# Expert 0's column selection and row gather placed ahead of the last tile's norm, and one ScalarE scaling placed later

## What is computed

```python
x = layer_norm(DN_ALPHA * x + merged @ w_out[l], ln1_g[l], ln1_b[l])
moe = grouped_moe(x, w_router, b_router, w_gate, w_up, w_down)
x = layer_norm(DN_ALPHA * x + moe, ln2_g[l], ln2_b[l])

# grouped_moe
gates = shared_group_router(xt, w_router, b_router)     # two of 16 are not zero for a token
for e in range(N_EXPERTS):
    h = jax.nn.silu(xt @ w_gate[e]) * (xt @ w_up[e])     # 1024 -> 512
    out = out + gates[:, e:e + 1] * (h @ w_down[e])      # 512 -> 1024
```

## Time and profile before

| | |
|---|---|
| median of 3 runs | 828.04 us (827.35 to 828.05) |
| profiled execution | 828.57 us, its span 826.9 us |
| TensorE busy | 814.5 us (99%) |
| VectorE busy | 574.3 us (69%) |
| ScalarE busy | 454.9 us (55%) |
| GpSimd busy | 82.7 us (10%) |
| memory read, written | 163.49 MB, 16.30 MB |

### The profile page before, as it was taken

One profiled execution on the slowest core, in us unless ns is written; L12 is line 12 of the kernel. 1 busy time (PEld: TensorE's weight loads), 2 busy tenths in 40 slices (PEclk: granted clock), 3 DMA queues, 4 the chain that ended last, 5 costly groups with the idle time before them and its releaser, 6 DMA issues.

```text
span 826.9 us, 11020 instructions
## 1 busy us (share of the span) xinstructions
PE 814.5 (99%) x3809; PEld 677.9 (82%) x3809; DVE 574.3 (69%) x672; ACT 454.9 (55%) x462; POOL 82.7 (10%) x78
## 2 busy tenths in 40 slices
PE   9999999999999999999999999999999999999995
PEld 8888888888888888888888888888888888888873
DVE  5877445434557885431455688899899898999857
ACT  5655524434466663333233333588787888878742
POOL 1000000100000000000000000633111011000037
PEclk9999999999999999999999999999999999999998
DMA  7332334553233323334432926599999999999592
GB/s 228 89 103 84 102 91 146 197 178 101 76 102 101 101 82 114 88 101 132 154 95 76 352 107 255 173 329 413 410 371 405 399 398 381 402 390 395 224 349 102
DMA packets 112358, 173.51 MB, mean 210 GB/s; under 512 B 7418, under 2 KB 90019, under 8 KB 100550
## 3 DMA queue, kind: packets, MB, share of 16 engines
q1 hardware_dynamic: 106502, 159.80, 54.4%
q0 software_dynamic: 5824, 13.30, 4.4%
HBM read 163.49 MB, written 16.30 MB: 217 GB/s over the span
## 4 chain that ended last, share of the span: by engine, by line
PE 92%; DMA 3%; DVE 3%; SPq 1%; issue 0%; ACT 0%; DVEq 0%; ACTq 0%; POOLq 0%
PE psA L717 8%; PE psA L719 8%; PE psA L718 8%; PE psA L904 7%; PE psA L906 7%; PE psA L905 7%; PE psB L717 6%; PE psB L718 6%; PE psB L719 6%; PE psB L931 3%; PE psB L930 3%; PE psB L929 3%; PE psD L718 2%; PE psD L717 2%; PE psC L718 2%; PE psC L717 2%
## 5 line engine op out<-in xcount | busy, mean ns | idle before, releaser
L1649 DVE TENSOR_TENSOR elo<-est,ehi 128x2048 fp32r<-128x2048 f32 x94 | 212.0, 2287 | 24.9 <-ACT ehi L1247 24.3
L1247 ACT ACTIVATE ehi<-est 128x2048 fp32r<-128x2048 f32 x94 | 178.9, 1922 | 52.8 <-DMA est<-in_w_exp_down_dram 32.0
L1434 DVE TENSOR_TENSOR wlo<-wst,whi 128x1024 fp32r<-128x1024 f32 (+1 forms) x75 | 93.8, 1251 | 84.9 <-ACT whi L1074 84.3
L1074 ACT ACTIVATE whi<-wst 128x1024 fp32r<-128x1024 f32 (+1 forms) x75 | 80.8, 1078 | 77.0 <-PE psB L719 30.7
L904 PE MATMUL psA<-ehi,xe_hi 128*128 128x512 f32 x256 | 101.4, 396 | 0.0
L906 PE MATMUL psA<-ehi,xe_lo 128*128 128x512 f32 x256 | 99.9, 390 | 0.0
L905 PE MATMUL psA<-elo,xe_hi 128*128 128x512 f32 x256 | 99.6, 389 | 0.0
L717 PE MATMUL psB<-xT_hi,whi 128*128 128x512 f32 x208 | 81.0, 390 | 0.0
L719 PE MATMUL psB<-xT_hi,wlo 128*128 128x512 f32 x208 | 80.9, 389 | 0.0
L718 PE MATMUL psB<-xT_lo,whi 128*128 128x512 f32 x208 | 80.9, 389 | 0.0
L906 PEld LDWEIGHTS psA<-ehi,xe_lo 128*128 128x128 f32 x256 | 48.0, 188 | 10.3
(11 more groups left out here) (372 smaller groups left out, 1535.6 us busy)
## 6 DMA issues: line engine op xcount, KB each, us to landing
est<-in_w_exp_gate_dram SPq DMA_DIRECT2D x32, 1024.0 KB, 11.0
est<-in_w_exp_up_dram SPq DMA_DIRECT2D x32, 1024.0 KB
est<-in_w_exp_down_dram SPq DMA_DIRECT2D x32, 1024.0 KB, 12.8
wst<-in_w_in_dram SPq DMA_DIRECT2D x59, 512.0 KB, 3.9
wst<-in_w_branch_r_dram SPq DMA_DIRECT2D x8, 640.0 KB, 4.3
ys<-zero POOLq DMA_DIRECT2D x8, 512.0 KB, 2.9
wst<-in_w_branch_a_dram SPq DMA_DIRECT2D x8, 512.0 KB, 3.6
o_st<-in_w_out_dram SPq DMA_DIRECT2D x8, 512.0 KB, 4.3
```

The source lines that it names most:

```text
L1074: A(whi[p][:, 0:K, :], wst[p][:, 0:K, :], ACT.Copy).then_inc(w_hi, 1)
L1247: A(ehi[s][:], est[s][:], ACT.Copy).then_inc(gu_hi if s < 4 else d_hi, 1)
L1434: V.tensor_tensor(wlo[p][:, 0:K, :], wst[p][:, 0:K, :], whi[p][:, 0:K, :], ALU.subtract).then_inc(w_lo, 1)
L1649: V.tensor_tensor(elo[s][:], est[s][:], ehi[s][:], ALU.subtract).then_inc(gu_lo if s < 4 else d_lo, 1)
```

## The change

On VectorE, only expert 0's share of `keys` is made first, then `first_by`, and only then the two halves of tile 3's norm, with the shares of experts 1 to 3 between and behind them. The two low parts of expert 0's rows come earlier. On TensorE, each half of the gather takes tiles 0 to 2 for all four k and then tile 3 for all four; the picks of experts 1 and 2 stand one quarter later; there are 12 and 2 warming matmuls for 14 and 6. In block 1, VectorE makes `hb` before two weight remainders, and the row remainder between them. On ScalarE, the scaling of block 0's output stands behind `hidden_round(2)`.

```diff
             pe.wait_ge(gu_hi, 1)
-            warm(14, psC[1][:, 1, :])
+            warm(12, psC[1][:, 1, :])
...
-            warm(6, psB[0])
+            def first_rows(k, t):
+                return pe.matmul(psC[0][:, k // 4, (k % 4) * P:(k % 4 + 1) * P], x1[:, t, k * P:(k + 1) * P],
+                                 first_by[:, t, :], start=(t == 0 and k % 4 == 0),
+                                 stop=(t == TT - 1 and k % 4 == 3))
+
+            warm(2, psB[0])
             pe.wait_ge(x1_done, TT - 1)
-            pe.wait_ge(x1_half, 1)
-            for k in range(KD):
-                if k == 4:
-                    pe.wait_ge(x1_done, TT)
-                for t in range(TT):
-                    if k == 0:
-                        pe.wait_ge(first_done, t + 1)
-                    mm = pe.matmul(psC[0][:, k // 4, (k % 4) * P:(k % 4 + 1) * P], x1[:, t, k * P:(k + 1) * P],
-                                   first_by[:, t, :], start=(t == 0), stop=(t == TT - 1))
-                if k == 3:
-                    mm.then_inc(x0_t, 1)
+            for h, (done, count) in enumerate(((x1_half, 1), (x1_done, TT))):
+                for k in range(4 * h, 4 * h + 4):
+                    for t in range(TT - 1):
+                        if k == 0:
+                            pe.wait_ge(first_done, t + 1)
+                        first_rows(k, t)
+                pe.wait_ge(done, count)
+                if h == 0:
+                    pe.wait_ge(first_done, TT)
+                else:
                     pe.wait_ge(by_done, 1)
                     picks(1)
-            mm.then_inc(xe_t, 1)
-            gate_up(0, first=True, parts=range(1))
+                for k in range(4 * h, 4 * h + 4):
+                    mm = first_rows(k, TT - 1)
+                mm.then_inc((x0_t, xe_t)[h], 1)
+            gate_up(0, first=True, parts=range(2))
             pe.wait_ge(by_done, 2)
             picks(2)
-            gate_up(0, first=True, parts=range(1, 2))
+            gate_up(0, first=True, parts=range(2, 3))
             rows_t(1, 1, xe_landed[1], 16)
             pe.wait_ge(by_done, 3)
             picks(3)
-            gate_up(0, first=True, parts=range(2, 4))
+            gate_up(0, first=True, parts=range(3, 4))
...
             def turn(b):
                 e_round(b + 1, 0)
                 e_round(b + 1, 1)
-                if b == 2:
-                    act.wait_ge(lists_landed, 16)
-                    act.wait_ge(y_evac, 2)
-                    A(yb[0][:], yb[0][:], ACT.Copy, scale=lists[:, 0, 2:3].bitcast(F32)).then_inc(y0_scaled, 1)
                 silu(b)
...
                 hidden_round(b)
+                if b == 2:
+                    act.wait_ge(lists_landed, 16)
+                    act.wait_ge(y_evac, 2)
+                    A(yb[0][:], yb[0][:], ACT.Copy, scale=lists[:, 0, 2:3].bitcast(F32)).then_inc(y0_scaled, 1)
...
-            for e in range(4):
-                ins = V.tensor_scalar(keys[:, e, :], sel[:, :, e], -1000.0, 1000.0, ALU.mult, ALU.add)
-            chain.link(ins)
-
-            spread_half(TT - 1, 0, x1_half)
+            chain.link(V.tensor_scalar(keys[:, 0, :], sel[:, :, 0], -1000.0, 1000.0, ALU.mult, ALU.add))
             dve.wait_ge(pos_done, 1)
...
-            for e in range(4):
-                V.tensor_tensor(keys[:, e, :], keys[:, e, :], at_pos[:, :, e], ALU.add).then_inc(key_done, 1)
+            V.tensor_tensor(keys[:, 0, :], keys[:, 0, :], at_pos[:, :, 0], ALU.add).then_inc(key_done, 1)
             dve.wait_ge(key_done, 1)
             for t in range(TT):
                 V.tensor_scalar(first_by[:, t, :], slots[:], keys[:, 0, t:t + 1], None, ALU.is_equal
                                 ).then_inc(first_done, 1)
+            spread_half(TT - 1, 0, x1_half)
+            for e in range(1, 4):
+                ins = V.tensor_scalar(keys[:, e, :], sel[:, :, e], -1000.0, 1000.0, ALU.mult, ALU.add)
+            chain.link(ins)
             spread_half(TT - 1, 1, x1_done)
+            for e in range(1, 4):
+                V.tensor_tensor(keys[:, e, :], keys[:, e, :], at_pos[:, :, e], ALU.add).then_inc(key_done, 1)
             listed(1)
+            rows_half(0)
             V.tensor_copy(pos[:], at_pos)
...
-            rows_half(0)
+            rows_half(1)
             paid = [r16[6], r16[7]]
...
             ins.then_inc(dest_done, 1)
-            rows_half(1)
             listed(2)
             listed(3)
...
             e_rest(0, 5)
+            hidden(1)
             e_rest(2, 0)
+            rows_rest(2)
             e_rest(2, 1)
-            hidden(1)
-            rows_rest(2)
             e_rest(2, 2)
```

More of the change, by code:

```diff
@@ L1810, in picked, with rows_half @@
                                 None, ALU.add).then_inc(pick_done, 1)
-            for e in range(4):
-                V.tensor_tensor(keys[:, e, :], keys[:, e, :], at_pos[:, :, e], ALU.add).then_inc(key_done, 1)
+            def rows_half(q):
+                dve.wait_ge((x0_h, xe_h)[q], 1)
+                V.tensor_tensor(xe_lo[:, 4 * q:4 * q + 4], psC[0][:, q, :].rearrange("p (k c) -> p k c", c=P),
+                                xe_hi[:, 4 * q:4 * q + 4], ALU.subtract).then_inc((x0_l, xe_l)[q], 1)
+            V.tensor_tensor(keys[:, 0, :], keys[:, 0, :], at_pos[:, :, 0], ALU.add).then_inc(key_done, 1)
             dve.wait_ge(key_done, 1)
@@ L1839, in _ @@
             chain.link(V.tensor_scalar(dest[:], rowsum[:], -1.0, None, ALU.add))
-            def rows_half(q):
-                dve.wait_ge((x0_h, xe_h)[q], 1)
-                V.tensor_tensor(xe_lo[:, 4 * q:4 * q + 4], psC[0][:, q, :].rearrange("p (k c) -> p k c", c=P),
-                                xe_hi[:, 4 * q:4 * q + 4], ALU.subtract).then_inc((x0_l, xe_l)[q], 1)
-            rows_half(0)
+            rows_half(1)
             paid = [r16[6], r16[7]]
```

## The result

The changed kernel took 831.01 us (median of 15 runs, 828.19 to 833.01); the kernel before, run beside it, 828.16 us (15 runs, 827.11 to 831.92). The ratio is 1.003, with a 95% interval of 1.0019 to 1.0041: 2.9 us slower, where 1.2 us faster than 828.04 was forecast. The profiled execution took 831.01 us, its span is 829.3 us.

The account below looks back on a forecast made before the run. TensorE, 92% of the chain that ended last, was taken to bound the kernel. A gather 1.36 us earlier less 0.05 gave 1.3: the median from 828.04 to 826.7, rounded to 826.8 for thin covers; range 825.7 to 828.3.

Parts of the forecast that it names:

- The gather: TensorE ahead of expert 0: first gather matmul 1.36 us earlier, tile 3's norm covered, first product at 518.2 instead of 519.56.
- the fillers' cost in time: TensorE around the position matmuls: two and four fewer warming matmuls cost nothing, so long as the clock stays.
- the sets of columns: VectorE's 0/1 columns for experts 2 and 3 end at 523.7; expert 2's picks have 0.8 us of cover.
- 1.36 - 0.05: Sum passed on to the end: 1.36 us from the earlier gather less 0.05 booked at expert 1's remainder, 1.3 us.
- What is late next: Expert 1's rows and weight remainders on VectorE: first remainder ends 536.44, wanted 536.43, cover about zero; 0.05 us booked.
- Everything later in that chain has 0.5 us or more: VectorE's chain behind expert 1's first weight remainder: every later step has at least 0.5 us of cover.
- rival B: Lead partly eaten by VectorE's chain or late weights: TensorE stalls 0.3 to 1.3 us, 827.1 to 828.1; chance 0.20.
- TensorE's busy time is whole in the later stretches: Argument against a TensorE stall on late VectorE work or weights: no idle time in later stretches; no size given.
- ScalarE's scale: Scaling of block 0's output, 1.14 us, put behind block 2's hidden-row rounding: its waiters have over 20 us; worth nothing.
- Block 1's order: VectorE makes `hb` ahead of two remainders; without that, ready 548.6 against 548.4 wanted, a fifth of the lead lost.
- D: Clock falls from 508.2 to 510.9; at 1.2 GHz the gather takes 14.6 for 7.3 us, 834 in all; chance 0.08.
- C: At the final norm, better-falling transfers shorten the 2.80 us wait for weights: up to 0.7 us more, 826.0; chance 0.12.

Follow-up runs that it names:

- SwiGLU early: Changed kernel with VectorE's tables for the last two blocks behind the loop and block 0's SwiGLU ahead of ScalarE's copy of expert 1's rows: 827.59 us, ratio 0.9988.
- changed, fillers back: Changed kernel with 16 and 3 warming matmuls instead of 12 and 2: 829.41 us, ratio 1.0011.
- changed, gather part alone: Changed kernel with only expert 0's columns and gather ahead of the norm; ScalarE's scale and VectorE's block-1 order as before: 829.49 us, ratio 1.0015.
- before, longer tables: Kernel before with the last eight comparisons of VectorE's tables for the last two blocks made twice, 1.7 us more work: 829.44 us, ratio 1.0017.
- changed, tables moved: Changed kernel with VectorE's 0/1 tables for the last two blocks (`last_by`, `prev_by`) moved behind the loop, after block 5's `hb`: 828.0 us, ratio 0.9996.

## Why the prediction was wrong, step by step

**The gather, the fillers' cost in time, the sets of columns: right.** First gather matmul 1.25 behind the position matmul as forecast, expert 0 at 8.57 (forecast 8.5), no wait inside the gather. The forecast 1.36 - 0.05 came out as 1.31 at expert 0.

**"What is late next": half right.** Expert 1's first product starts at 531.36 though the one before it left off at 530.81 + 0.23 = 531.04: 0.32 us of the lead are lost there. What TensorE waited for is not VectorE's low part but ScalarE's read of block 0's gate, since the product writes over it. ScalarE's timeline after the change:

```profile
528.33 1.03 ACT L1357 ACTIVATE xe_hi<-psC 128x1024 fp32r<-128x1024 f32 x1 [1.88 <-PE psC L888]
529.37 1.28 ACT L1312 ACT_TABLE_LOAD   x1
530.66 0.60 ACT L1312 ACTIVATE sg<-psA 128x512 f32<-128x512 f32 x1
```

530.66 + 0.60 = 531.26, 0.10 ahead of 531.36. The prediction followed the copy of expert 1's rows and not what stands behind it in ScalarE's queue. That the kernel with SwiGLU early has no such gap (its list of waits has none from issue) bears this out. The remainders of 534.15 started at 534.71, 0.56 later than worked out (the position matmul itself came 0.44 later), and TensorE did not wait there. The end of the first of them follows from the prediction's own numbers as 534.15 + 2.23 = 536.38, not 536.44; that makes a cover of 0.05 us where the prediction had about zero, and the 0.05 us that it booked was not lost.

**The step that failed** is the sentence "Everything later in that chain has 0.5 us or more", with its brother in rival B, "TensorE's busy time is whole in the later stretches". A whole busy time says that nothing is late; it does not say by how much. The prediction read the covers of remainders and hidden rows up to 549.71 and not beyond. Block 5's `hb` had 0.42 us, the lead alone was forecast at 1.3. So even with nothing late on VectorE the lead would have met its end there. The second half of the failed step is a cost put at nothing: VectorE's weight remainders became later, and `hb` with them, 1.69 us. Together it was more than the lead: the wait is the lead, plus the lateness of `hb`, less the cover, lead and lateness counted from the first position matmul (the lead at 603.79 for the changed kernel, the product ahead of the wait):

| kernel | lead | `hb` late | sum less 0.42 | wait |
|---|---|---|---|---|
| changed | 0.91 | 1.69 | 2.18 | 2.09 |
| changed, fillers back | 0.96 | 1.26 | 1.80 | 1.69 |
| changed, scale back | 0.18 | 1.77 | 1.53 | 1.42 |
| changed, gather part alone | 0.17 | 1.01 | 0.76 | 0.66 |
| changed, block 1 back | 0.15 | 0.97 | 0.70 | 0.60 |
| before, longer tables | 0.04 | 1.70 | 1.32 | 1.22 |
| before, scale late and block 1 | -0.04 | 0.49 | 0.03 | none |
| changed, tables moved | 0.96 | -1.03 | -0.49 | none |

The sum is about 0.1 too high wherever there is a wait; the kernel before with the scale late, with a sum of 0.23 and 0.12 idle, fits too. In itself this is little more than arithmetic: it holds as long as TensorE loses nothing between the two marks. What shows the cause are the two experiments that move one term alone: `hb` late without any part of the change (1.22 of wait, 1.3 us of time), and the cover widened with all of the change in place (no wait, the 3 us gone).

**Why `hb` is 1.69 late: shown in part.** The chain of waits of the changed kernel, 538 to 640:

```profile
548.14 11.02 DVE elo L1655 x5
559.31 12.40 DMA est<-in_w_exp_down_dram
571.73 1.93 ACT ehi L1253
573.68 2.30 DVE elo L1655
576.14 13.24 DMA est<-in_w_exp_down_dram
589.40 1.93 ACT ehi L1253
...
593.81 14.93 DMA est<-in_w_exp_down_dram
608.76 1.93 ACT ehi L1253
610.71 2.29 DVE elo L1655
```

Read it as a wheel: a remainder frees a weight buffer, SyncE starts the next 1 MB load into it, ScalarE rounds what lands, VectorE makes the remainder. It turns once in some 17 us (559.31, 576.14, 593.81), and TensorE is in none of these rows, so a lead of TensorE does not hurry it. VectorE came to it late: `hb` of block 0 starts 0.43 later than before, counted from the position matmul (534.11 - 510.12 against 533.24 - 509.68). The kernel before with the scale late has the same wheel in its chain of waits, with loads of 11.93, 13.19 and 14.83 us for 12.40, 13.24 and 14.93 here. Counted from the end of `sel`, the first load starts 0.43 later here and lasts 0.47 longer, the two others last 0.05 and 0.10 longer. This makes 1.05, and `hb` is 1.69 late here and 0.65 there, 1.04 apart. The length of the last load is not what is new.

Which part of the change brings it? With the gather in place, the four profiles give: both placements old 1.01, only the scale late 0.97, only block 1's order new 1.77, both 1.69. So beside the 1.01 of the gather, block 1's new order makes `hb` 0.72 to 0.76 later, and the scale nothing. Without the gather it is otherwise: scale alone 0.65, both placements 0.49. The parts don't simply add up, and each figure is from one profile; why they interact stays open.

**ScalarE's scale, "worth nothing by itself": right alone, wrong with the rest.** Alone it is not shown to change the time (0.9997), though it makes block 5's `hb` 0.65 late. With the gather and block 1's new order the late place saves 0.50 to 0.70 us of waiting near 568, since the lists land later; neither pair of medians shows that as time (831.01 with it late, 829.25 with it back; 828.0 and 827.8 with the tables moved). The prediction let the scale wait "for `lists`" at its old time. GpSimd's first indirect load is 1.15 later, about the 1 us forecast, but the load of `lists` is issued at 553.76 instead of 550.45, 2.87 later counted from the position matmul.

**Block 1's order:** near by it does more than forecast: without it TensorE waits 0.38 us at 550, and the lead to block 2 falls from 0.91 to 0.16, where the prediction gave it a fifth of the lead. The wait is not for `hb` but for the rows' low part `xe_lo` behind it. Further on its price appears, the 0.72 us by which block 5's `hb` is later. Both run into the same cover: with the new order the wait for `hb` is 2.09, with the old one 0.60, and the kernel with the old one is the faster (829.24 against 831.01).

**The rivals.** B named the right kind (VectorE and the weights behind full DMA engines), and even a buffer freed later as the price of pulling the hidden row ahead, which the forecast itself put at nothing; the place and the size were wrong, 0.3 to 1.3 us for a wait of 2.09 and a loss of 3.96. D said that the clock would fall at 508 to 511. In one profile of 14 it fell at 511 and cost the gather 1.63 us, where the prediction priced the whole gather at double (7.3); in four it fell between 505 and 509, at no cost. That the 6 runs over 832 are executions with both falls of the clock, and the 3 under 829.2 with none, is argued from the three groups and from the kernel with fillers (829.41 against 831.01), not shown in a profile of one of them. That a wait elsewhere also lowers the clock (1.61 us behind 2.09 of waiting) was no part of any rival. C did not happen as forecast: the last norm's wait for its weights fell from 2.80 to 1.70, but the norm began 2.40 later, at 810.02. Nor need the 1.09 us that the end gives back be due to the change: in the kernel before with only the tables moved, block 15 begins within 0.1 us of its old place and the end is 0.97 shorter. The end of the profile of before is a long one; over the 14 profiles it takes 44.83 to 48.09 us, and what sets it was not found.

**Still open.** With the tables moved TensorE keeps 1.0 us to block 15, but the median gains nothing over the kernel before (828.0 against 827.85). Some of it goes at the last block, by its chain of waits:

```profile
785.39 6.99 DMA est<-in_w_exp_down_dram
792.40 1.93 ACT dl_hi L1393
794.36 2.29 DVE dl_lo L1967
796.65 0.61 DVE h_lo L1979
797.30 0.50 PE psA L1003
```

where TensorE has waited 0.5 us for `h_lo`, behind the last down weights. The fillers are not the answer there (827.85 with, 827.59 without). In the one profile each, both spans are about 1 us under the one of before (825.5 and 826.0 against 826.9), but these profiles flatter: their executions took 827.15 and 827.67, 0.85 and 0.18 under their kernels' medians, and the one of before 828.57, 0.53 above its own.

The best kernel is the one with the tables moved and the SwiGLU early, 827.59 us, ratio 0.9988 (0.9979 to 0.9996); moving the tables alone in the kernel before gives 827.63. Nothing of the gather's lead is seen in the time; what was gained was gained by the wider cover.

## What to carry to other kernels

Before a lead is booked, list for each later wait how long the thing waited for had been ready, on every block up to the end, and stop the lead at the smallest cover: here 0.42 us, 110 us behind the edit. An engine that is 100% busy over a stretch shows that nothing is late, not that anything is early. Where a small job without a near deadline (the two tables, 2.7 us; the earlier trace rows has their first use 190 us later) stands ahead of one with a deadline on the same engine, move it before anything else: here that was worth 3 us to the changed kernel, and to the kernel before 0.5.

## What the runs showed of the chip that was not expected

A wait of 2.09 us cost 3.96, some 1.6 of it by the clock: it fell behind the wait, and from 624.74 on the matmuls stood 0.43 apart instead of 0.23 until 626.87. Waits of 0.60, 0.66, 1.22, 1.42 and 1.69 in other kernels here left the granted clock of 620 to 640 at 1.00, and cost 0.24 to 0.26 more than their length. The same code ahead of the gather, with the same 0.57 of 2 us busy, kept its clock in one profile and lost 1.63 us in another. In four more profiles the clock fell a little earlier, behind a stretch without a gap, and cost nothing. One profile shows only one of these cases. The range of the runs does not show them either (4.8 us in both kernels, 827.11 to 831.92 and 828.19 to 833.01); what differs is where the runs crowd, 6 of 15 over 832 against none.
